# Reordering the second block's mixers in a 256-token transformer kernel

## The reference

```python
h = rms_norm_2(x, mix_norm[l])
z = h @ w_in[l]                                    # 1024 x 6752
(na_q, na_k, na_v, gq, gk, gv, gr, gfl, gbl, c_q, c_kv, k_rope, gates) = split_cols(z, IN_SPLITS)

qa = rms_norm_2(na_q, na_q_norm[l]); ka = rms_norm_2(na_k, na_k_norm[l])   # per head of 64
y_na = neighborhood_attention(qa, ka, na_v, na_rpb[l])                     # 8 heads

g_f = log_sigmoid(gfl @ gla_gf_up[l] + gla_gf_bias[l]) / 16
g_b = log_sigmoid(gbl @ gla_gb_up[l] + gla_gb_bias[l]) / 16
o_gla = gla_bidirectional(gq, gk, gv, g_f, g_b)    # 4 heads, chunks of 64, forward and backward
y_gla = rms_norm_2(o_gla, gla_out_norm[l]) * silu(gr)

# mla_attention: 4 heads, 128 nope + 64 rope columns for q and k, 128 for v
q  = rms_norm_2(c_q, cq_norm) @ w_uq               # 256 x 768, the query expansion
kv = rms_norm_2(c_kv, ckv_norm) @ w_ukv            # 256 x 1024, the key/value expansion
k  = concatenate([k_nope, k_rope for every head])
q, k = rms_norm_2(q, q_norm), rms_norm_2(k, k_norm)
q, k = [each with its last 64 columns rotated (rope)]
y_mla = blocked_softmax_attention(q, k, v, 192 ** -0.5)

gt = sigmoid(gates.reshape(B, S, 3, 1024))
mixed = gt[0] * (y_na @ w_br_na[l]) + gt[1] * (y_gla @ w_br_gla[l]) + gt[2] * (y_mla @ w_br_mla[l])
x = x + mixed @ w_out[l]
```

## Time and profile before

| | |
|---|---|
| median of 3 timed runs | 2225.98 us (2224.84 to 2226.51) |
| the profiled execution, its own time | 2227.1 us |
| its span in the trace | 2225.3 us |
| PE busy | 2087.3 us, 94% |
| PE weight loads (beside the products) | 1694.5 us, 76% |
| VectorE busy | 1260.5 us, 57% |
| ScalarE busy | 1035.6 us, 47% |
| GpSimd busy | 140.3 us, 6% |
| mean granted clock of PE | 0.963 of full speed |

### The profile page before, as it was taken

How to read it: one execution, slowest core, us unless ns; L and a number is a source line. 1 busy time by engine, 2 the same in 40 slices (tenths; PEclk the granted TensorE clock), 3 DMA queues, 4 the chain that set the end, 5 groups by cost and what they waited for, 6 DMA issues and landing times.

```text
span 2225.3 us, 26765 instructions
## 1 busy us (share of the span) xinstructions
PE 2087.3 (94%) x9932; PEld 1694.5 (76%) x9932; DVE 1260.5 (57%) x1822; ACT 1035.6 (47%) x1635; POOL 140.3 (6%) x148
## 2 busy tenths in 40 slices
PE   6989799999799999999988989999999989899999
PEld 6865688877678878887767678888888767677887
DVE  4646654577655555555755655555455666655544
ACT  5544643455454454444553435445344445444443
POOL 0000100000000000002120100000000311110000
PEclk9978999999989999999889799999999999999999
DMA  7420465553345555555532345555555453434552
GB/s 261 149 90 28 134 204 189 189 180 105 95 142 189 189 168 192 188 189 159 171 105 66 129 146 175 189 189 172 188 189 170 131 179 100 142 107 158 189 189 95
DMA packets 247640, 346.12 MB, mean 156 GB/s; under 512 B 28180, under 2 KB 177496, under 8 KB 247512
## 3 DMA queue, kind: packets, MB, share of 16 engines
q1 hardware_dynamic: 246680, 342.92, 47.6%
q0 software_dynamic: 544, 1.29, 0.3%
q10 hardware_dynamic: 288, 0.21, 0.0%
HBM read 343.32 MB, written 2.33 MB: 155 GB/s over the span
## 4 chain that ended last, share of the span: by engine, by line
PE 43%; issue 6%; DVE 2%; ACT 1%; POOL 1%; DVEq 0%; ACTq 0%; POOLq 0%
PE bank L643 13%; PE bank L645 13%; PE bank L644 13%; PE bank L1210 1%; POOL o_buf L2347 1%; PE bank L578 1%; DVE w_lo L472 1%; PE bank L905 1%; PE bank L2672 0%; PE bank L2678 0%; ACT h_hi L1351 0%; PE bank L1069 0%; PE bank L2629 0%; PE bank L1019 0%; ACT w_hi L484 0%
## 5 line engine op out<-in xcount | busy, mean ns | idle before, releaser
L472 DVE TENSOR_TENSOR w_lo<-raw,w_hi 128x2048 fp32r<-128x2048 f32 (+5 forms) x480 | 739.9, 1561 | 402.7 <-ACT w_hi L484 402.2
L643 PE MATMUL bank<-w_hi,h_hi 128*128 128x512 f32 (+4 forms) x1936 | 768.3, 397 | 55.9 <-issue 16.6
L645 PE MATMUL bank<-w_hi,h_lo 128*128 128x512 f32 (+4 forms) x1936 | 752.9, 389 | 0.0
L644 PE MATMUL bank<-w_lo,h_hi 128*128 128x512 f32 (+4 forms) x1936 | 751.9, 388 | 0.0
L484 ACT CAST w_hi<-raw 128x2048 fp32r<-128x2048 f32 (+5 forms) x480 | 618.3, 1315 | 261.8 <-PE bank L645 260.6
L643 PEld LDWEIGHTS bank<-w_hi,h_hi 128*128 128x128 f32 x1936 | 372.1, 192 | 140.2 <-issue 20.7
L645 PEld LDWEIGHTS bank<-w_hi,h_lo 128*128 128x128 f32 x1936 | 371.0, 192 | 72.7
L644 PEld LDWEIGHTS bank<-w_lo,h_hi 128*128 128x128 f32 x1936 | 373.0, 193 | 67.1
L643 PE MATMUL bank<-w_hi,ff_hi 128*128 128x512 f32 x528 | 206.1, 390 | 0.0
L645 PE MATMUL bank<-w_hi,ff_lo 128*128 128x512 f32 x528 | 205.6, 389 | 0.0
L644 PE MATMUL bank<-w_lo,ff_hi 128*128 128x512 f32 x528 | 205.5, 389 | 0.0
(11 more groups left out here) (267 smaller groups left out, 1630.0 us busy)
## 6 DMA issues: line engine op xcount, KB each, us to landing
raw<-in_ffn_w SPq DMA_DIRECT2D x176, 512.0 KB, 4.5
raw<-in_w_in SPq DMA_DIRECT2D x52, 1024.0 KB, 5.4
raw<-in_ffn_w SPq DMA_DIRECT2D x44, 1024.0 KB, 4.9
raw<-in_ffn_wg SPq DMA_DIRECT2D x44, 512.0 KB, 4.0
raw<-in_ffn_wu SPq DMA_DIRECT2D x44, 512.0 KB, 5.0
raw<-in_ffn_wd SPq DMA_DIRECT2D x22, 1024.0 KB, 4.8
raw<-in_od_w_in SPq DMA_DIRECT2D x12, 1024.0 KB, 5.1
raw<-in_w_out SPq DMA_DIRECT2D x8, 1024.0 KB, 5.1
```

The costliest lines, as they stand in the source:

```text
L472: dve.tensor_tensor(lo_[:, cs], raw_[:, cs], hi[:, cs].bitcast(F32), ALU.subtract).then_inc(*dve_did.up())
L643: pe.matmul(out, x_hi, u.hi[:, k, cols_], start=start, stop=False)
L644: pe.matmul(out, x_hi, u.lo[:, k, cols_], start=False, stop=False)
L645: return pe.matmul(out, x_lo, u.hi[:, k, cols_], start=False, stop=stop)
```

## The change

It has four parts. All of the arithmetic stays, but for a factor of 1/192 that moves into another constant.

**The gate.** `start_gates` takes the marks that its products wait for. Gate 0 is started ahead of the neighborhood attention, bound to the end of the projection, so its steps follow the projection's as fillers there. The latents' sums of squares move behind the log-sigmoid of the linear attention. Only half of gate 1 is started then; its other half comes in `latent`. The unit order puts the units of w_uq between the two halves.

**The linear attention.** The state updates stand ahead of the scores. The turning of both latents and the rotation of the key's rope columns (`latent_turn`) stand between the scores and the output. `og` lies in another buffer (`gain`).

**The latent attention.** The query expansion comes right behind the linear attention's output, then the second half of gate 1, then the turning of `og`, then the key/value expansion. The rope of the queries comes ahead of all query transposes, and `r_q` is computed in one operation less on VectorE.

**The end.** Branch 2 begins with the two heads that are ready first, the two row tiles in turn. The first half of `o_buf` is turned after six steps of it, and four products of w_out come ahead of turning the second half.

The diff, cut to its core:

```diff
-GLA_FILLS = (4, 8, 16, 4, 8)
+GLA_FILLS = (4, 8, 12, 4)
...
-        units += gates[1] + gemm_units(a["mla_w_uq_2"][l], chunked(MLA_H * MLA_QK))
+        half = len(gates[1]) // 2
+        units += gates[1][:half] + gemm_units(a["mla_w_uq_2"][l], chunked(MLA_H * MLA_QK)) + gates[1][half:]
...
+        def both_tiles(h, k0, u, nk, c, n, pair, there, evac):
+
+            tiles = [tile_steps(tt, h, k0, u, nk, c, n, pair, there, evac) for tt in range(TT)]
+            while True:
+                for steps in tiles:
+                    if next(steps, None) is None:
+                        return
+                    yield True
...
+            start_gates(after)
             attention(groups, flat(o_buf[:, 0, :]), after, lambda i: (4, 3))
             y_there = attended["o"]
-            while fillers:
-                fill()
+            assert len(fillers) == 1
             prepare()
-            rstd_heads(*((z[:, :, ZC[name]:ZC[name] + 2 * P].unsqueeze(2), r, 1, 2 * P,
-                          sq[:, :, m * 2 * P:(m + 1) * 2 * P]) for m, (name, r) in enumerate(
-                              (("cq", rs[:, 24:26]), ("ckv", rs[:, 26:28])))))
-            start_gates()
             start_branch(0, y_there)
-            start_gates()
+            start_gates(after, chunked(D)[0:1])
...
             before = marks()
-            fill(GLA_FILLS[3])
-            og = tmp[:, :, 0:512]
+            turned_ahead = latent_turn(l, begun)
+            while fillers:
+                fill()
+            prepare()
+            og = gain[:, 0, :].rearrange("p (t n) -> p t n", t=TT)
...
+            gemm(blocks_of(cq_hi, cq_lo, 2), 2, chunked(MLA_H * MLA_QK),
                  to_sbuf(lambda tt, c, n: q[:, tt, c:c + n], rs_of(24)), split[0])
...
+            start_gates(split[0], chunked(D)[1:2])
+            while fillers:
+                fill()
+            linear_there = turn_linear()
...
+            gemm(blocks_of(oT_lo, oT_lo[:, 2:4, :], 2), 2, chunked(MLA_H * (MLA_NOPE + MLA_V)), evac_kv, split[1])
             kv_there = marks()
+            turn_rope(l, qv[:, :, :, MLA_NOPE:MLA_QK], MLA_H, 0, Marks(q_there.pe, q_squared, q_there.dve, q_there.pool),
+                      kT[:, :, :].rearrange("p (t a) n -> p t (a n)", t=TT))
+            q_turned = marks()
             start_branch(1, linear_there)
-            start_gates()
+            start_gates(split[0])
...
-            q_reduced = dve_did.now()
+            power(r_q, TT * MLA_H, 1.0, None, EPS * MLA_QK)
+            q_powered = pool_did.now()
             fill(2)
             gq = col_of[("mla_q", l)] % P
             to_T(MLA_H, lambda h, tt: qv[:, tt, h, 0:MLA_NOPE], lambda b, n: qT[:, b:b + n, :],
-                 scale=lambda b: cols[:, 1, gq:gq + 1], after=q_there)
-            turn_rope(qv[:, :, :, MLA_NOPE:MLA_QK], MLA_H, 0, Marks(q_there.pe, q_squared, q_reduced, q_there.pool), sq)
-            q_turned = marks()
+                 scale=lambda b: cols[:, 1, gq:gq + 1], after=q_turned)
+            to_T(MLA_H, lambda h, tt: qv[:, tt, h, MLA_NOPE:MLA_QK], lambda b, n: qT[0:MLA_ROPE, 4 + b:4 + b + n, :],
+                 width=MLA_ROPE, after=q_turned)
...
-            start_branch(2, attended["o"])
-            while fillers:
-                fill()
+            start_branch(2, Ready([attended["outs"][0], attended["o"]], 2))
...
-            latent(l, gated_linear(l))
-            by_half = [Marks(pe_did.now(), act_did.now(), dve_did.now(), mixed[(TT - 1, c)]) for c in (0, 512)]
-            acc = out_banks()
-            for k0, after in zip((0, KD // 2), by_half):
-                groups, steps = half_of_o(k0, after)
+            last.clear()
+            latent(l, *gated_linear(l))
+            o = attended["o"]
+            while (TT - 1, 0) not in last:
+                fill()
+            fill(2)
+            turned = []
+            for k0 in (0, KD // 2):
+                groups, steps = half_of_o(k0, Marks(o.pe, o.act, o.dve, last[TT - 1, k0 * P]))
                 for _ in steps:
                     pass
-                for _ in out_steps(acc, h_in, k0, groups[-1], add_x):
-                    pass
+                turned.append(groups[-1])
+                if k0 == 0:
+                    while fillers:
+                        fill()
+                    acc = out_banks()
+                    products = out_steps(acc, h_in, 0, turned[0], add_x)
+                    for _ in range(4):
+                        next(products)
...
```

## The result

The changed kernel takes 2192.3 us, against 2226.2 us before. The ratio is 0.9839, with a 95% interval of 0.9819 to 0.9860, so it is faster by 1.6%. Forecast were 2186.5 us and a range of 2172 to 2206: the time is in the range, and 6 us above the forecast.

What follows compares the result with a forecast made beforehand. TensorE's waits and lower clock were taken as the bound. Terms 10.5 - 1.0 + 8.1 + 5.6 gave 23.2 us a mixer, 46.4 for two, 39.4 after 3.5 a mixer for the clock: 2186.5 us, range 2172 to 2206.

Steps and rivals of the forecast that it cites:

- What bounds the kernel: Whole kernel: TensorE, busy 94% of the span, is a queue of products, shortened only where it waits or runs at lower clock.
- Part A: Gate started behind the projection, its steps filling neighborhood attention and the time behind it: gain 10.5 us a mixer.
- wait on a bank: Sign against the prediction: it is wrong if a wait on a bank or on `up` appears.
- Part B: Linear attention, states ahead of scores and latents turned early: a 2.7 us wait ahead of the output, loss 1.0 us.
- Part C: From the end of the linear attention's output products to the latent scores: 57.9 us becomes 49.8, gain 8.1 us a mixer.
- All three waits: New waits of 1.8 us within gate 1 and 3.8 ahead of key transposes; 2.2 ahead of query transposes, where 4.3 stood.
- rival 3: VectorE, slowed where it shares time with POOL, leaves Part C 3 us a mixer: 2190, or 2197 with clock; chance 0.12.
- set aside for the clock: Allowance for low-clock stretches behind the new waits: 3.5 us a mixer, from bounds of 0 and 10.
- Part D: Mixer's end, output turned ahead: waits of 1.4, 1.0, 1.6 and 1.6 covered, gain 5.6 us a mixer.
- Rival 1: Clock stays up: no new low stretch, and the first mixer's low latent scores go too; 2171 to 2179, chance 0.13.
- Rival 2: Clock falls ahead of the key transposes and stays low through the scores in both mixers: 2201, chance 0.17.

Runs made afterwards that it cites:

- less_add: Changed kernel with GpSimd adding only the first 8 of 512 columns of branch 1 to the mixed output, leaving out part of the computation: 2185.1 us.
- keys_first: Changed kernel with VectorE's scaling of the keys issued ahead of the three filler steps behind the query transposes: 2209.9 us.
- two_moves: Changed kernel with the linear attention's output multiplied behind the query expansion and one filler step issued ahead of qe and ke: 2177.4 us.
- og_late: Changed kernel with the two multiplications of the linear attention's output issued behind the query expansion's copies instead of ahead: 2186.8 us.
- keys_wait_moved: keys_first with one wait added: PE waits for the turned keys' copies ahead of the two filler steps before the latent scores: 2203.8 us.

## Why the prediction was right, and where its steps were not

- *What bounds the kernel.* Right: PE's waits and its clock. Every wait that was forecast is there, each at its place and with its releaser, and those that were to go are gone.
- *Part A.* Right to 1.1 us a mixer up to `up`'s product (19.6 and 18.6 forecast, 20.3 and 19.7 measured). Its last sentence failed: "The latents' sums, moved behind log_sigmoid, lie under 8 steps, 11 us, where before PE waited for nothing." PE does not wait for the sums; what stands behind them in ScalarE's and VectorE's queues comes 2.8 us later, and among it is the operation that empties a bank. The stretch came out 3.1 and 6.1 us too long: 1.9 and 3.1 of wait and the rest low clock. In the second mixer that stands behind the bank wait; in the first it stands behind the wait ahead of `up`'s product (1134.7 to 1141.5), so the sums are not its cause. It is one of the two largest errors, and a wait on a bank is what the text had named as showing it wrong.
- *Part B.* 19.3 against 18.8 in the first mixer, with waits of 3.0 against 2.7. In the second 20.9, with a low stretch.
- *Part C.* All three waits came. Forecast 1.8, 2.2 and 3.8 us, measured 3.8, 1.3 and 4.4. The first was mis-sized: the low part was placed behind og's chain in VectorE's queue, and the cast of the same weights (1.9 us) behind ScalarE's copy, which waits for the same chain, was left out. GpSimd's additions make 1.9 of the third's 4.4 (less_add); rival 3 had that mechanism. With low stretches of 6.8 us together in each mixer the loss against the forecast is 4.7 and 5.5 us, where 3.5 had been set aside for the clock of the whole mixer.
- *Part D.* 5.6 forecast, 7.3 and 6.5 measured between the scores and the turning of x (0.9 of it clock in the first mixer). A part of the surplus may be overlap: neighbouring products of 128x512 start 0.23 us apart and last 0.39, so a gap costs an estimated 0.16 more than the wait that the list shows. No experiment sets this apart.
- *The rivals.* Rival 1 was half right: the first mixer's low scores are gone (6.5 us), and the other low stretches are not. This was luck for the forecast, which had no such term: without it the time would be near 2199, 12 us above the forecast and still in the range. Rival 2 did not happen here, and keys_first shows its mechanism at full size: 7.6 us more a mixer in the scores behind a wait of 3.7. The scores that spoke for it in the kernel before began at full clock, which fell about 2.4 us into them. Of all mixers traced, 4 of 4 with that wait had low scores, 1 of 6 with a wait of 0.9 to 1.2 there, and none of 18 without one. The Trainium skill ("TensorE: Matmul & The Clock Gate", section on HAM oscillation) says that products which alternate with waits lose the clock again each time, and was cited as speaking against this change. In keys_first the trace agrees: the clock fell behind the wait of 3.7 us in both mixers. In the changed kernel the removal of waits outweighed the new ones, and the low time fell from 92 to 48 us.

The sum: 46.4 forecast for the two mixers without clock, 30.9 measured. The differences from the table, forecast less measured, are -1.8 (first row), -9.2, -3.0, -10.2, +6.6 and +2.7, which makes -14.9; the last 0.6 is rounding and the turning of qe and ke. 7 had been set aside. So the time is in the range because two errors of about 10 us, the stretch of the bank wait and Part C, were met in part by the 7 set aside and by the scores' 6.6.

What stays open: why the first mixer's scores were low in the trace of before and not in the second. A wait of about 1 us stands ahead of both, and no experiment sets it apart from chance. Nor was it settled why the changed kernel's timed runs lie further apart (2187.6 to 2195.0) than two_moves' (2175.9 to 2180.3).

## What to carry to other kernels

When a small piece of work is moved to a place where the main engine does not wait, follow what stands behind it in its own queues until something that the main engine needs: a bank, a cast, a low part. Price a wait by what runs behind it: in og_late 3.1 us less of wait ahead of plain weight products were worth 4.1 and 3.8 us, and in keys_first a wait of 3.7 us ahead of the scores cost 7.6 us more in the scores alone. A wait that must be had was better placed ahead of two steps of plain products, even though it got longer (keys_wait_moved). Which property of the scores matters, their width of 256 columns or another, no run shows.

## What the runs showed of the hardware

- A busy PE can stay at the lower clock. In keys_first it fell behind a wait of 3.7 us and stayed low for 20.5 us without a gap, through the rest of the 32 scores and nine 128x512 products behind them. In keys_wait_moved, with twelve such products behind a wait of 6.6 us, nine of them were slow and the clock was back 4.0 us behind the wait.
- VectorE beside GpSimd: a quarter low part took 0.67 us alone (less_add), and 1.0 and 1.4 us beside additions of 128x512 on GpSimd (the changed kernel).
